# Short group's attention first, heads loaded one stage ahead, pooling in half pieces shared by GpSimd and VectorE

## Chip, cores, metric

One NeuronCore of a Trainium2 chip runs the whole layer as one launch. The metric is device time in microseconds (us).

## What is computed

Two request groups, a short one of 1024 tokens and a long one of 2048, go through one encoder layer with shared weights. Cut to what matters here:

```
z = (rmsnorm(x) * (1 + sc1) + sh1) @ w_in
c_q, c_kv, k_pe, u = split(z)                          # 384, 256, 32, 512 columns
q = rmsnorm(c_q) @ w_uq ; kv = rmsnorm(c_kv) @ w_ukv    # 8 heads: 64 + 32 (rotated) per query, 64 + 64 per key
att = softmax(q k^T / sqrt(96)) v                       # per head, within a group
pool = (mean of u over a window of 2, 4, 8 or 16 tokens - u) @ w_pool * pool_scale
x = x + g1 * (concat(att, pool) @ w_out)
y = rmsnorm(x + g2 * expert_choice_ffn(rmsnorm(x) * (1 + sc2) + sh2))
```

The window means divide by the number of tokens really in the window, so the first and last eight tokens of a sequence have factors of their own.

## The kernel before, in words

The stages follow each other with a barrier of all engines between them: modulation, `in_proj`, `latent_proj`, attention of the long group, attention of the short group, output weights and projection, routing, experts, final norm. Every float32 operand is split into a high and a low half, and a product is three matmuls. Between stages data goes through DRAM: `s_qn`, `s_qr`, `s_kn`, `s_v` hold the projected heads, `s_kr` the rotated key part that all heads share, `s_ut` the pooling input, `s_diff` the pooling result.

**`latent_proj` (L512)** works through six blocks of 512 tokens. A block has 16 items in the order `ORDER` (L526): four each of k, q and v, and two pairs r, t (the rotated query part). TensorE (PE) computes an item into one of eight PSUM banks, ScalarE (ACT) writes its high half, VectorE (DVE) its low half, and SyncE (SP) stores it. SP's queue (L674) is in program order, and so is the work that its transfers do. Beside this GpSimd (POOL) pools the windows in twelve jobs (L635), two per block: SP fetches a piece of 1024 tokens with its margins, POOL adds neighbours in one to four doublings, scales, subtracts, mends the ends, and SP stores the result at two places of a block (L712): `store_diff` waits until POOL has finished the job, then comes `fetch` of the job after next. Stores of items stand behind these waits in SP's queue.

**`attention` (L850)** is called for `g = 1` (long, two heads resident in SBUF, loops over four pairs) and then for `g = 0` (short, four heads resident, two rounds). SP first issues the loads of all resident heads (L985 to L992); PE waits for the first head's q and k (L1029, L1030). POOL writes three constant rows (L1224): row 96 of a head's tiles carries the row maxima through the score product. Then a pipeline runs in steps `s` of one 128-key tile against 512 queries: three score matmuls, `exp` and high half on ACT, low half on POOL, two value matmuls; PE also computes the next query block's maxima (`unit`), which DVE reduces. A block has 8 steps in the short group, 16 in the long one. After a block, at fixed steps of the next ones, its sums are finished: `sum_row` on ACT writes the row sums, SP's `fold` (L966) turns them by a small transfer, DVE's `inverse` (L1195) takes reciprocals and waits for that transfer, SP's `store_inverses` stores them, and `store` writes the output. In the short group `inverse` of block 0 comes at step 18 (`INV = 10`, L864). DVE executes in order, so everything behind `inverse` waits with it. SP's `body` (L994) starts only after the loads above it are issued.

Of the kernel before, what the change touches and what calls it, by code (L numbers as in the profile page):

```python
# [22 lines left out]
F32 = mybir.dt.float32  # L23
# [487 lines left out]

def latent_proj(nc, w, keep):  # L512
# [11 lines left out]
    SPAN = min(SEQS)  # L524
# [6 lines left out]
    PER = len(ORDER)  # L531
    SIMPLE = [i for i, (kind, _) in enumerate(ORDER) if kind in "kqv"]
    SLOT = {"q": 0, "r": NQ, "k": NQ + RT, "v": NQ + RT + KT}
    with ExitStack() as ctx:
# [10 lines left out]
        out = m.sb("out", [P, SLOTS, 2, BANK], F32R)  # L545
        prod = m.sb("prod", [P, 2, BANK])
# [22 lines left out]
        edge_in = m.sem("edge_in")  # L569
        pads_set = m.sem("pads_set")  # L570
# [47 lines left out]
        @block.gpsimd  # L618
        def _(pool):
            m.clear_last(pool)  # L620
            step = sequence(summed)
            pads = sequence(pads_set)

            def set_pads(n):

                first, last = ends_of(n)
                if first:
                    pads(nc.gpsimd.memset(u[:, n % 2, 0:PAD], 0.0))
                if last:
                    pads(nc.gpsimd.memset(u[:, n % 2, PAD + SPAN:], 0.0))  # L630

            for n in range(2):
                set_pads(n)
            pool.wait_ge(edge_in, 16)
            for n, (g, c, o) in enumerate(JOBS):  # L635
                x = u[:, n % 2]
                pool.wait_ge(u_in[n % 2], 16 * (n // 2 + 1))
                done = step(nc.gpsimd.tensor_tensor(sums[:, 0, 1:SPAN + 2 * PAD], x[:, 0:SPAN + 2 * PAD - 1],
                                                    x[:, 1:SPAN + 2 * PAD], ALU.add))
                for lev in range(1, c + 1):  # L640
                    r = 1 << (lev - 1)
                    lo, hi = 2 * r, SPAN + 2 * PAD - 2 * r + 1
                    src, dst = sums[:, (lev - 1) % 2], sums[:, lev % 2]
                    pool.wait_ge(summed, done)
                    done = step(nc.gpsimd.tensor_tensor(dst[:, lo:hi], src[:, lo - r:hi - r], src[:, lo + r:hi + r],
                                                        ALU.add))
                total = sums[:, c % 2]
                pool.wait_ge(summed, done)
# [3 lines left out]
                if first:  # L652
                    done = step(nc.gpsimd.tensor_tensor(ends[:, 0:PAD], total[:, PAD:2 * PAD], edge[:, c, 0:PAD], ALU.mult))
                if last:
                    done = step(nc.gpsimd.tensor_tensor(ends[:, PAD:], total[:, SPAN:SPAN + PAD], edge[:, c, PAD:], ALU.mult))
                done = step(nc.gpsimd.tensor_scalar(sums[:, (c + 1) % 2, PAD:PAD + SPAN], total[:, PAD:PAD + SPAN],
                                                    1.0 / WINDOWS[c], None, ALU.mult))
                pool.wait_ge(summed, done)
                a, b = PAD * first, SPAN - PAD * last
                done = step(nc.gpsimd.tensor_tensor(diff[:, n % 2, a:b], sums[:, (c + 1) % 2, PAD + a:PAD + b],  # L660
                                                    x[:, PAD + a:PAD + b], ALU.subtract))
                if first:
                    done = step(nc.gpsimd.tensor_tensor(diff[:, n % 2, 0:PAD], ends[:, 0:PAD], x[:, PAD:2 * PAD],
                                                        ALU.subtract))
                if last:
                    done = step(nc.gpsimd.tensor_tensor(diff[:, n % 2, SPAN - PAD:], ends[:, PAD:], x[:, SPAN:SPAN + PAD],
                                                        ALU.subtract))
                pool.wait_ge(summed, done)
                pool.sem_inc(diff_ready, 1)
                if n + 2 < len(JOBS):  # L670
                    set_pads(n + 2)

        @block.sync
        def _(sp):  # L674
# [9 lines left out]
            def fetch(n):  # L684

                g, c, o = JOBS[n]
                a, b = max(o - PAD, 0), min(o + SPAN + PAD, SEQS[g])
                if n >= 2:
                    sp.wait_ge(diff_ready, n - 1)
                sp.wait_ge(pads_set, sum(sum(ends_of(i)) for i in range(n + 1)))  # L690
# [9 lines left out]
            load(0)  # L700
            sp.dma_start(qraw[:], w["w_uq"][0].rearrange("(k p) n -> p k n", p=P)).then_inc(q_in, 16)
# [4 lines left out]
            for n in range(2):  # L706
                fetch(n)
            load(1)
            for b in range(NB):
# [21 lines left out]
                if b + 2 < NB:  # L731
                    sp.wait_ge(ready, (b + 1) * PER)
                    load(b + 2)
            for slot in range(SLOTS):
                sp.wait_ge(stored[slot], 16 * NB)
            for i in range(2):
                sp.wait_ge(diff_stored[i], 16 * len(JOBS) // 2)
# [69 lines left out]
        def _(dve):  # L807
            for n, (src, g, dst) in enumerate(pieces()):
                dve.wait_ge(w_hi_done, n + 1)
                nc.vector.scalar_tensor_tensor(dst[1], src, g, dst[0].bitcast(F32), ALU.mult,  # L810
                                               ALU.subtract).then_inc(w_lo_done, 1)
            dve.wait_ge(tabs_in, 2 * 16 * (P // ROPE))
            for b in range(NB):
# [3 lines left out]
                for n, (kind, i) in enumerate(ORDER):  # L817
                    q = b * PER + n
# [31 lines left out]
def attention(nc, w, keep, g):  # L850
# [18 lines left out]
    with ExitStack() as ctx:  # L869
        m = Pools(nc, ctx, f"att{g}")  # L870
        q = m.sb("q", [P, HU, 2, S], F32R)
        k = m.sb("k", [P, HU, 2, S], F32R)
        v = m.sb("v", [P, HU, NT, 2 * VD], F32R)
# [16 lines left out]
        kpe_in = m.sem("kpe_in")  # L890
# [58 lines left out]
        def _(sp):  # L949
            def load_qk(n, i):  # L950
                for dst, src in ((q[0:NOPE, i], w["s_qn"]), (q[NOPE:QK, i], w["s_qr"]), (k[0:NOPE, i], w["s_kn"])):
# [3 lines left out]
            def load_v(n, i):  # L955
                src = w["s_v"][t0:t0 + NT, :, bass.ds(n * 2 * VD, 2 * VD)]
                sp.dma_start(v[:, i].bitcast(F32), src.rearrange("t p c -> p t c")).then_inc(v_in[i], 16)
# [27 lines left out]
            load_qk(0, 0)  # L985
            for i in range(HU):
                sp.dma_start(k[NOPE:QK, i].bitcast(F32), w["s_kr"][:, :, tokens]
                             .rearrange("l r t -> r l t")).then_inc(kpe_in, 16)
# [18 lines left out]
            over_heads(sp, body)  # L1007
            store(ITERS, -1)
# [7 lines left out]
        def _(pe):  # L1016
            def unit(i, j, u):
# [3 lines left out]
                nc.tensor.matmul(m_ps[u % MB][:, :], q[0:QK, i, 0, at:at + P], k[0:QK, i, 0, cols(kb)],  # L1021
# [7 lines left out]
            pe.wait_ge(qk_in[0], 48)  # L1029
            pe.wait_ge(kpe_in, 16 * HU)  # L1030
# [6 lines left out]
            pe.wait_ge(rows_set, 4)  # L1037

            def scores(it, s):
# [6 lines left out]
                k_hi, k_lo = (k[0:QK + 1, h, l, kt * P:(kt + 1) * P] for l in range(2))  # L1046
                q_hi, q_lo = (q[0:QK + 1, h, l, cols(j)] for l in range(2))
# [4 lines left out]
            def values(it, s):  # L1052

                b, kt, h, j = at(s)
                if kt == 0:
                    if j == 0:
                        pe.wait_ge(v_in[h], 16 * (it + (1 if b >= 0 else 0)))
# [3 lines left out]
                for a in range(2):  # L1061
                    mm = nc.tensor.matmul(o_ps[b % 2][:, :], v[:, h, kt, :], pr[:, s % RING, a, :],  # L1062
# [11 lines left out]
            def body(it, last):  # L1074
                for s in range(PER):
# [5 lines left out]
                    if not (last and b == NG - 1):  # L1081
                        i, nj = after(b)
                        for u in UNITS[kt]:
                            if u == 0 and nj == 0:
                                pe.wait_ge(qk_in[i], 48 * (it + (2 if i == 0 else 1)))
# [12 lines left out]
        def _(act):  # L1098
            def max_row(i, j):
                nc.scalar.activation(q[QK:QK + 1, i, 0, cols(j)], m_ps[MB - 1][0:1, :], ACT.Copy).then_inc(row_done, 1)  # L1100
# [1153 lines left out]
def build(nc, w):  # L2254
# [6 lines left out]
    with ExitStack() as ctx:  # L2261
# [7 lines left out]
        latent_proj(nc, w, keep)  # L2269
        for g in (1, 0):  # L2270
            attention(nc, w, keep, g)
# [32 lines left out]
    "s_rden": [HEADS, TOKENS],  # L2304
    "s_diff": [DP // P, P, TOKENS],
# [61 lines left out]
```

## Time and profile before

| | |
|---|---|
| median of 3 runs | 4012.92 us (4011.62 to 4013.34) |
| the profiled execution | 4013.25 us, of which its span 4011.4 us |
| PE busy | 3628.6 us, 90% of the span |
| DVE, ACT, POOL busy | 2025.0, 1890.8, 1346.4 us |
| granted PE clock, mean | 0.946 |

Times in the trace run from the first instruction; the span ends with the last, and 1.85 us lie around it. The stages that the change touches stand at 489.7 to 700.6 us (`latent_proj`), 700.6 to 1519.2 us (long attention) and 1519.2 us to about 1755 us (short attention).

### The profile page before, as it was taken

Reading aid. Unit: us, or ns where it says so; the run is one execution under the profiler, and the core shown is the slowest. Engines: PE = TensorE matmul, PEld = TensorE weight load, DVE = VectorE, ACT = ScalarE, POOL = GpSimd, SP = SyncE. Lnnn points to the kernel's source line nnn. Section 1 sums busy time; section 2 is a strip of 40 time slices with the busy share of each in tenths; the row PEclk is TensorE's granted clock in tenths of the full one; section 3 lists DMA queues with packets and bytes.
Section 4 is the critical chain, followed back from the end, with each engine's and each line's share of the span. In section 5 each row is a group of like instructions: output and inputs, shape, how many; then the busy total and the mean of one; then the engine's idle time right before and its main releaser. Section 6 shows DMA issues by size and latency. Waiting matters only on the chain. (4 is left out here: it accounts for less than half of the span.)

```text
span 4011.4 us, 53884 instructions
## 1 busy us (share of the span) xinstructions
PE 3628.6 (90%) x18873; PEld 3093.1 (77%) x18873; DVE 2025.0 (50%) x3111; ACT 1890.8 (47%) x3258; POOL 1346.4 (34%) x1008
## 2 busy tenths in 40 slices
PE   8799897799999997969995599999999999999991
PEld 1799876577777775747773499999999999999991
DVE  0333254688888886842225554444444444444443
ACT  0444232688888895843321234344444434443433
POOL 0212067688988897852221000000000000000000
PEclk9899999899999998989996699999999999999995
DMA  7422399422222205235642344444444455444537
GB/s 253 146 100 94 110 364 365 87 43 43 43 44 43 44 6 114 60 105 153 181 146 89 105 137 152 147 145 150 148 152 152 156 157 157 152 146 151 157 100 272
DMA packets 350510, 538.89 MB, mean 134 GB/s; under 512 B 33782, under 2 KB 234742, under 8 KB 347386
## 3 DMA queue, kind: packets, MB, share of 16 engines
q1 hardware_dynamic: 326332, 448.60, 35.6%
q0 software_dynamic: 13824, 50.34, 5.2%
q10 hardware_dynamic: 10176, 37.75, 2.3%
q8 instruction: 90, 1.47, 0.2%
q14 instruction: 88, 0.72, 0.1%
HBM read 394.08 MB, written 142.46 MB: 134 GB/s over the span
## 5 line engine op out<-in xcount | busy, mean ns | idle before, releaser
L1229 POOL TENSOR_TENSOR att_pr<-att_e,att_pr 128x512 fp32r<-128x512 f32 x640 | 813.1, 1294 | 146.0 <-ACT att_pr L1116 135.6
L1982 POOL DMA_INDIRECT s_x<-moe_ye,moe_to_add x48 | 90.9, 1893 | 1440.1 <-DVE moe_ye L2169 1430.4
L1160 DVE TENSOR_REDUCE att_mx<-att_m_ps 128x1 f32<-128x512 f32 x640 | 423.2, 682 | 111.8 <-PE att_m_ps L1021 102.3
L2117 DVE TENSOR_TENSOR keep_wl<-keep_raw,keep_wh 128x1024 fp32r<-128x1024 f32 x380 | 440.0, 1221 | 34.1 <-ACT keep_wh L2071 34.1
L2071 ACT ACTIVATE keep_wh<-keep_raw 128x1024 fp32r<-128x1024 f32 x380 | 370.0, 1045 | 126.0 <-PE moe_d_ps L2048 126.0
L1062 PE MATMUL att_o_ps<-att_pr,att_v 128*128 128x512 f32 x1280 | 408.6, 400 | 4.8 <-POOL att_pr L1229 4.6
L1116 ACT ACTIVATE att_pr<-att_e 128x512 fp32r<-128x512 f32 x640 | 402.8, 629 | 18.3 <-issue 2.7
L1110 ACT ACTIVATE att_e<-att_s_ps 128x512 f32<-128x512 f32 x640 | 379.7, 593 | 64.7 <-PE att_s_ps L1050 20.1
L1182 DVE TENSOR_TENSOR att_acc_ps<-att_acc_ps,att_e 128x512 f32<-128x512 f32 x544 | 375.0, 689 | 17.2 <-ACT att_e L1110 11.0
L2097 ACT ACTIVATE moe_silu<-moe_a_ps 128x384 f32<-128x384 f32 x128 | 63.0, 492 | 645.7 <-PE moe_u_ps L2021 645.7
L2019 PE MATMUL moe_a_ps<-moe_xh,keep_wh 128*128 128x384 f32 x1024 | 345.9, 338 | 3.0 <-DVE moe_xl L2122 3.0
L2020 PE MATMUL moe_a_ps<-moe_xl,keep_wh 128*128 128x384 f32 x1024 | 345.2, 337 | 0.0
L2021 PE MATMUL moe_a_ps<-moe_xh,keep_wl 128*128 128x384 f32 x1024 | 345.0, 337 | 0.0
L2021 PE MATMUL moe_u_ps<-moe_xh,keep_wl 128*128 128x384 f32 x1024 | 344.1, 336 | 0.0
L2019 PE MATMUL moe_u_ps<-moe_xh,keep_wh 128*128 128x384 f32 x1024 | 344.1, 336 | 0.0
L2020 PE MATMUL moe_u_ps<-moe_xl,keep_wh 128*128 128x384 f32 x1024 | 344.1, 336 | 0.0
L2152 DVE TENSOR_TENSOR moe_hf<-moe_u_ps,moe_silu 128x384 f32<-128x384 f32 x128 | 71.3, 557 | 537.1 <-ACT moe_silu L2097 537.1
L2046 PE MATMUL moe_d_ps<-keep_wh,moe_hh 128*128 128x512 f32 x768 | 311.6, 406 | 0.0
L2048 PE MATMUL moe_d_ps<-keep_wh,moe_hl 128*128 128x512 f32 x768 | 303.9, 396 | 0.0
L2047 PE MATMUL moe_d_ps<-keep_wl,moe_hh 128*128 128x512 f32 x768 | 303.8, 396 | 0.0
L1062 PEld LDWEIGHTS att_o_ps<-att_pr,att_v 128*128 128x128 f32 x1280 | 242.4, 191 | 67.0 <-POOL att_pr L1229 12.3
L1021 PE MATMUL att_m_ps<-att_k,att_q 96*128 96x512 f32 x640 | 236.5, 411 | 58.7 <-DMA att_k<-s_kr 58.7
(266 smaller groups left out, 7720.9 us busy)
## 6 DMA issues: line engine op xcount, KB each, us to landing
keep_raw<-w_gate SPq DMA_DIRECT2D x64, 1024.0 KB, 5.3
keep_raw<-w_up SPq DMA_DIRECT2D x64, 1024.0 KB, 7.8
keep_raw<-w_down SPq DMA_DIRECT2D x64, 1024.0 KB, 6.7
ada_wa<-w_ada SPq DMA_DIRECT2D x12, 2048.0 KB, 9.8
s_ct<-inp_ct SPq DMA_DIRECT2D x24, 640.0 KB, 3.0
prj_ct<-s_ct SPq DMA_DIRECT2D x6, 2560.0 KB, 16.6
s_kn<-prj_out SPq DMA_DIRECT2D x24, 512.0 KB, 12.2
s_qn<-prj_out SPq DMA_DIRECT2D x24, 512.0 KB, 11.9
```

The source lines that it names most:

```text
L1062: mm = nc.tensor.matmul(o_ps[b % 2][:, :], v[:, h, kt, :], pr[:, s % RING, a, :], start=(kt == 0 and a == 0), stop=(kt == NT - 1 and a == 1))
L1110: nc.scalar.activation(e[:, s % RING, :], s_ps[s % 2][:, :], ACT.Exp, scale=SCALE).then_inc(exp_done, 1)
L1116: nc.scalar.activation(pr[:, s % RING, 0, :], e[:, s % RING, :], ACT.Copy).then_inc(hi_done, 1)
L1160: nc.vector.tensor_reduce(mx[:, u % CB, u // CB:u // CB + 1], m_ps[u % MB][:, :], AX, ALU.max).then_inc(max_part, 1)
L1182: step = nc.vector.tensor_tensor(acc_ps[:, :], acc_ps[:, :], e[:, s % RING, :], ALU.add)
L1229: nc.gpsimd.tensor_tensor(pr[:, s % RING, 1, :], e[:, s % RING, :], pr[:, s % RING, 0, :].bitcast(F32), ALU.subtract).then_inc(lo_done, 1)
L2019: nc.tensor.matmul(out, hi, xh[:, k, :], start=(k == 0), stop=False)
L2020: nc.tensor.matmul(out, hi, xl[:, k, :], start=False, stop=False)
L2021: mm = nc.tensor.matmul(out, lo, xh[:, k, :], start=False, stop=(k == KD - 1))
L2046: nc.tensor.matmul(out, h_hi, wh[:, c % 2, k, :], start=(k == 0), stop=False)
L2071: nc.scalar.activation(wh[:, s, part, :], raw[:, s, part, :], ACT.Copy).then_inc(w_hi_done, 1)
L2117: nc.vector.tensor_tensor(wl[:, s, part, :], raw[:, s, part, :], wh[:, s, part, :].bitcast(F32), ALU.subtract).then_inc(w_lo_done, 1)
```

## The change

1. Attention runs for the short group first, then the long one.
2. A tile `ahead0` takes q and k of the short group's first head; `latent_proj` loads it on SP's queue after the third block. A tile `ahead1` takes q, k and v of the first two heads of the long group; the short group's attention loads it behind its own three remaining heads, before its `body`. PE no longer waits at the start of either attention.
3. The constant rows are written to DRAM once (`s_rows`) and loaded per head, in place of POOL's memsets.
4. Pooling works on 24 pieces of 512 tokens, four places per block; POOL only adds (the last addition writes `diff`) and mends the ends, DVE scales and subtracts in one instruction per piece, ahead of the item at that place. The first two fetches come before the query weights.

```diff
+HEAD_LOADS = 8
+def load_heads(sp, w, g, n, heads, which, sem, values=True):
+    S = SEQS[g]
+    NT = S // P
+    tokens = slice(STARTS[g], STARTS[g] + S)
+    for i in which:
+        q, k, v = heads[i]
+        for dst, src in ((q[0:NOPE], w["s_qn"][:, n + i, :, tokens]), (q[NOPE:QK], w["s_qr"][:, n + i, :, tokens]),
+                         (k[0:NOPE], w["s_kn"][:, n + i, :, tokens]), (k[NOPE:QK], w["s_kr"][:, :, tokens])):
+            sp.dma_start(dst.bitcast(F32), src.rearrange("l r t -> r l t")).then_inc(sem, 16)
+        for dst, row in ((k[QK:QK + 1, 0], 1), (k[QK:QK + 1, 1], 0), (q[QK:QK + 1, 1], 0)):
+            sp.dma_start(dst.bitcast(F32), w["s_rows"][row:row + 1, 0:S]).then_inc(sem, 16)
+        if values:
+            sp.dma_start(v.bitcast(F32), ...).then_inc(sem, 16)
 def latent_proj(nc, w, keep):
-    SPAN = min(SEQS)
+    SPAN = BANK
+    JOBS_PER = len(JOBS) // NB
+    POINTS = [PER * (i + 1) // JOBS_PER - 2 for i in range(JOBS_PER)]
...
             def store_diff(n):
                 sp.wait_ge(diff_ready, n + 1)
+                sp.wait_ge(ends_ready, n + 1)
...
-                    if at in (PER // 3, 2 * PER // 3):
-                        n = 2 * b + int(at > PER // 2)
+                    if at in POINTS:
+                        n = JOBS_PER * b + POINTS.index(at)
                         store_diff(n)
                         if n + 2 < len(JOBS):
                             fetch(n + 2)
...
+                if b == SEQS[0] // BANK:
+                    sp.wait_ge(w_lo_done, ALL_PIECES)
+                    for slot in range(SLOTS):
+                        sp.wait_ge(stored[slot], 16 * b)
+                    load_heads(sp, w, 0, 0, head_tiles(keep, 0, None), range(1), ahead_in, values=False)
...
+            def difference(n):
+                dve.wait_ge(total_ready, n + 1)
+                nc.vector.scalar_tensor_tensor(diff[:, n % 2, a:b], diff[:, n % 2, a:b], 1.0 / WINDOWS[c],
+                                               u[:, n % 2, PAD + a:PAD + b], ALU.mult, ALU.subtract).then_inc(diff_ready, 1)
...
                 for n, (kind, i) in enumerate(ORDER):
+                    if n in POINTS:
+                        difference(JOBS_PER * b + POINTS.index(n))
 def attention(nc, w, keep, g):
-            load_qk(0, 0)
...
-            load_v(0, 0)
-            for i in range(1, HU):
-                load_qk(i, i)
-                load_v(i, i)
+            if g == 0:
+                load_v(0, 0)
+            for i in range(READY, HU):
+                load_heads(sp, w, g, 0, heads, (i,), rest_in[i])
+            if g == 0:
+                load_heads(sp, w, 1, 0, head_tiles(keep, 1, None), range(2), ahead_in)
...
-            pe.wait_ge(qk_in[0], 48)
-            pe.wait_ge(kpe_in, 16 * HU)
...
-            for row, value in ((k[QK:QK + 1, :, 0, :], 1.0), (k[QK:QK + 1, :, 1, :], 0.0), (q[QK:QK + 1, :, 1, :], 0.0)):
-                nc.gpsimd.memset(row.bitcast(F32), value).then_inc(rows_set, 1)
 def build(nc, w):
-        latent_proj(nc, w, keep)
-        for g in (1, 0):
-            attention(nc, w, keep, g)
+        with ExitStack() as ahead:
+            tile(ahead, "ahead0", [P, 4 * SEQS[0]], F32R, side="right")
+            latent_proj(nc, w, keep)
+            tile(ahead, "ahead1", [P, 2 * (4 * SEQS[1] + SEQS[1] // P * 2 * VD)], F32R, side="right")
+            for g in range(2):
+                attention(nc, w, keep, g)
```

SP's queue at the start of the short group's attention, before (`att_v`, `att_q`, `att_k` are the resident heads, `att_rden` the folded sums):

```order
L952 DMA att_q<-s_qn 64x2x1024
L952 DMA att_q<-s_qr 32x2x1024
L952 DMA att_k<-s_kn 64x2x1024
L957 DMA att_v<-s_v 128x8x128
L962 DMA s_att<-att_att 64x512
L973 DMA att_rden<-att_den 128x1x4
L980 DMA s_rden<-att_rden 128x4
```

and the end of the same loads now (`keep_ahead` is the tile filled ahead, `s_rows` the constant rows):

```order
L544 DMA att_v<-s_v 128x8x128
L540 DMA keep_ahead<-s_qn 64x2x2048
L540 DMA keep_ahead<-s_qr 32x2x2048
L540 DMA keep_ahead<-s_kn 64x2x2048
L540 DMA keep_ahead<-s_kr 32x2x2048
L542 DMA keep_ahead<-s_rows 1x2048 x3
L544 DMA keep_ahead<-s_v 128x16x128
L1030 DMA s_att<-att_att 64x512
L1041 DMA att_rden<-att_den 128x1x4
L1048 DMA s_rden<-att_rden 128x4
```

Two long heads (the second has the rows of the first) now stand between the short group's last head and the first store of results and the first fold.

In `latent_proj`, SP's queue after the third block holds, now, the first short head between the load of block 4 and the stores of block 3:

```order
L774 DMA s_qr<-prj_out 128x2x512
L721 DMA prj_ct<-s_ct 128x4x1280
L540 DMA keep_ahead<-s_qn 64x2x1024
L540 DMA keep_ahead<-s_qr 32x2x1024
L540 DMA keep_ahead<-s_kn 64x2x1024
L540 DMA keep_ahead<-s_kr 32x2x1024
L542 DMA keep_ahead<-s_rows 1x1024 x3
L774 DMA s_kn<-prj_out 128x2x512
```

Before, a store of `s_kn` followed the load of block 4 at once.

## Rows read from the trace of the kernel before

**Rows 1.** The page, busy time of each engine.

```profile
PE 3628.6 (90%) x18873; PEld 3093.1 (77%) x18873; DVE 2025.0 (50%) x3111; ACT 1890.8 (47%) x3258; POOL 1346.4 (34%) x1008
```

**Rows 2.** Busy times by stretch, latent projection: span; engines; PEclk, DMA share, GB/s.

```profile
515.00:545.00 30.00, 30.00 (x125) 24.59 (x125) 14.63 (x19) 7.11 (x12) 23.96 (x17) 0.93 1.03 400
545.00:549.00 4.00, 4.00 (x19) 3.34 (x18) 3.30 (x3) 2.69 (x5) 3.44 (x5) 1.00 0.31 122
549.00:680.00 131.00, 128.41 (x566) 106.02 (x566) 73.93 (x97) 38.00 (x66) 93.65 (x73) 1.00 1.03 398
685.00:690.00 5.00, 0.00 (x0) 0.00 (x0) 1.13 (x1) 0.31 (x1) 4.92 (x2) 0.50 0.11 43
690.00:700.00 10.00, 0.00 (x0) 0.00 (x0) 0.00 (x0) 0.00 (x0) 0.37 (x3) 0.50 0.83 316
```

**Rows 3.** Timeline of SP's queue, end of the latent projection.

```profile
679.68 1.17 SPq L730 DMA_DIRECT2D s_qn<-prj_out  x1
690.45 0.34 SPq L697 DMA_DIRECT2D s_diff<-prj_diff  x1
...
694.69 1.21 SPq L730 DMA_DIRECT2D s_qr<-prj_out  x1
700.57 0.66 SPq L952 DMA_DIRECT2D att_q<-s_qn  x1
```

**Rows 4.** Tile s_qn, the store issued at 679.68 us alone.

```profile
DMA to landing us min/median/max: 11.2/11.2/11.2
```

**Rows 5.** Timeline of PE around both attention starts.

```profile
680.70 0.39 PE L772 MATMUL prj_ps<-prj_ct,prj_wq 128*128 128x512 f32 x1
720.73 9.52 PE L1021 MATMUL att_m_ps<-att_k,att_q 96*128 96x512 f32 x16 [39.64 <-DMA att_k<-s_kr]
...
1513.58 0.63 PE L1071 MATMUL att_o_ps<-att_acc_lo,att_ones 128*1 128x512 f32 x1
1533.22 4.74 PE L1021 MATMUL att_m_ps<-att_k,att_q 96*128 96x512 f32 x8 [19.02 <-DMA att_k<-s_kr]
```

**Rows 6.** Timeline of SP's queue, short group: first and last head load, first results.

```profile
1519.17 0.65 SPq L952 DMA_DIRECT2D att_q<-s_qn  x1
...
1546.13 0.60 SPq L957 DMA_DIRECT2D att_v<-s_v  x1
...
1563.80 0.53 SPq L962 DMA_DIRECT2D s_att<-att_att  x1
1568.02 0.54 SPq L973 DMA_DIRECT2D att_rden<-att_den  x1
...
1576.30 1.09 SPq L962 DMA_DIRECT2D s_att<-att_att  x1
```

**Rows 7.** Timeline of DVE, the short group's first inverse.

```profile
1572.55 0.17 DVE L1197 RECIPROCAL att_rden<-att_rden 128x4 f32<-128x4 f32 x1
```

**Rows 8.** Busy times by stretch while heads load, columns as in Rows 2.

```profile
701.00:740.00 39.00, 17.30 (x40) 10.30 (x41) 13.23 (x23) 6.16 (x10) 13.37 (x6) 0.53 1.00 216
1521.00:1560.00 39.00, 24.59 (x83) 17.45 (x84) 18.64 (x32) 15.19 (x26) 21.96 (x14) 0.67 1.00 214
1533.00:1546.60 13.60, 11.42 (x25) 7.07 (x26) 7.10 (x13) 3.63 (x6) 2.56 (x2) 0.50 1.07 236
```

**Rows 9.** DMA of the stretch 1519 to 1562 us: packets, MB, share.

```profile
q1 hardware_dynamic: 5952, 8.39, 91.6%
```

**Rows 10.** Tile att_rden in the short group: DVE's waits for the fold; issue to landing.

```profile
  DMA att_rden<-att_den: 8.3, 4
...
DMA to landing us min/median/max: 1.4/2.0/5.6
```

**Rows 11.** Lines L638, L810 and L834: ns min/median/max, first and last start.

```profile
L638 POOL TENSOR_TENSOR prj_sums<-prj_u x12: 1917/1918/1923, 518.8 to 675.7; 128x1039 f32<-128x1039 f32 x12
...
L810 DVE SCALAR_TENSOR_TENSOR prj_wk<-prj_kvraw,prj_gain,prj_wk x2: 747/750/753, 496.2 to 497.6; 128x512 fp32r<-128x512 f32 x2
...
L834 DVE TENSOR_TENSOR prj_qf<-prj_prod x12: 692/931/2747, 529.4 to 681.9; 128x512 f32<-128x512 f32 x12
```

More of the change, by code:

```diff
@@ L509, in _, with head_tiles @@
                     mm.then_inc(ct_ready, 1)
+HEAD_LOADS = 8
+def head_tiles(keep, g, left):
+    S = SEQS[g]
+    NT = S // P
+    size = 4 * S + (NT * 2 * VD if g else 0)
+    heads = []
+    for i in range(2 if g else 1):
+        x = keep[f"ahead{g}"][:, i * size:(i + 1) * size]
+        heads.append((x[:, 0:2 * S].rearrange("p (l t) -> p l t", l=2), x[:, 2 * S:4 * S].rearrange("p (l t) -> p l t", l=2),
+                      x[:, 4 * S:].rearrange("p (t c) -> p t c", t=NT) if g else left and left[2][:, 0]))
+    if left:
+        q, k, v = left
+        heads += [(q[:, i], k[:, i], v[:, i + 1]) for i in range(3)]
+    return heads
+def load_heads(sp, w, g, n, heads, which, sem, values=True):
+    S = SEQS[g]
+    NT = S // P
+    tokens = slice(STARTS[g], STARTS[g] + S)
[7 more added lines that the diff above has]
+        if values:
+            sp.dma_start(v.bitcast(F32), w["s_v"][TILE0[g]:TILE0[g] + NT, :, (n + i) * 2 * VD:(n + i + 1) * 2 * VD]
+                         .rearrange("t p c -> p t c")).then_inc(sem, 16)
 def latent_proj(nc, w, keep):
@@ L545, in latent_proj @@
         out = m.sb("out", [P, SLOTS, 2, BANK], F32R)
+        rows = m.sb("rows", [P, 2, max(SEQS) // P], F32R)
         prod = m.sb("prod", [P, 2, BANK])
@@ L569, in latent_proj @@
         edge_in = m.sem("edge_in")
+        ahead_in = m.sem("ahead_in")
+        rows_set = m.sem("rows_set")
+        rows_stored = m.sem("rows_stored")
+        total_ready = m.sem("total_ready")
+        ends_ready = m.sem("ends_ready")
         pads_set = m.sem("pads_set")
@@ L630, in set_pads @@
                     pads(nc.gpsimd.memset(u[:, n % 2, PAD + SPAN:], 0.0))
+            for i in range(2):
+                nc.gpsimd.memset(rows[:, i, :].bitcast(F32), float(i)).then_inc(rows_set, 1)
             for n in range(2):
@@ L637, in _ @@
                 pool.wait_ge(u_in[n % 2], 16 * (n // 2 + 1))
[L638 to L648, printed above, removed]
                 if n >= 2:
@@ L651, in _ @@
                 first, last = ends_of(n)
[L652 to L669, printed above, removed]
+                for lev in range(c + 1):
+                    r = 1 << lev >> 1
+                    lo, hi = 2 * r + (lev == 0), SPAN + 2 * PAD - 2 * r + (lev > 0)
+                    src = sums[:, (lev - 1) % 2] if lev else x
+                    before, behind = (src[:, lo - r:hi - r], src[:, lo + r:hi + r]) if lev else (src[:, lo - 1:hi - 1], src[:, lo:hi])
+                    if lev == c:
+                        cut = slice(PAD - lo, PAD - lo + SPAN)
+                        nc.gpsimd.tensor_tensor(diff[:, n % 2], before[:, cut], behind[:, cut], ALU.add).then_inc(total_ready, 1)
+                    else:
+                        done = step(nc.gpsimd.tensor_tensor(sums[:, lev % 2, lo:hi], before, behind, ALU.add))
+                        pool.wait_ge(summed, done)
@@ new lines, in _ @@
+                if first or last:
+                    pool.wait_ge(total_ready, n + 1)
+                for here, at, e0 in ((first, 0, 0), (last, SPAN - PAD, PAD)):
+                    if here:
+                        done = step(nc.gpsimd.tensor_tensor(ends[:, e0:e0 + PAD], diff[:, n % 2, at:at + PAD],
+                                                            edge[:, c, e0:e0 + PAD], ALU.mult))
+                        pool.wait_ge(summed, done)
+                        done = step(nc.gpsimd.tensor_tensor(diff[:, n % 2, at:at + PAD], ends[:, e0:e0 + PAD],
+                                                            x[:, PAD + at:2 * PAD + at], ALU.subtract))
+                        pool.wait_ge(summed, done)
@@ L700, in _ @@
             load(0)
+            for n in range(2):
+                fetch(n)
             sp.dma_start(qraw[:], w["w_uq"][0].rearrange("(k p) n -> p k n", p=P)).then_inc(q_in, 16)
@@ L705, in _ @@
             sp.dma_start(edge[:].rearrange("p a b -> p (a b)"), w["k_edge"].partition_broadcast(P)).then_inc(edge_in, 16)
-            for n in range(2):
-                fetch(n)
             load(1)
+            sp.wait_ge(rows_set, 2)
+            sp.dma_start(w["s_rows"].rearrange("l (p c) -> p l c", p=P), rows[:].bitcast(F32)).then_inc(rows_stored, 16)
             for b in range(NB):
@@ L811, in _ @@
                                                ALU.subtract).then_inc(w_lo_done, 1)
+            def difference(n):
+                c = JOBS[n][1]
+                first, last = ends_of(n)
+                a, b = PAD * first, SPAN - PAD * last
+                dve.wait_ge(total_ready, n + 1)
+                nc.vector.scalar_tensor_tensor(diff[:, n % 2, a:b], diff[:, n % 2, a:b], 1.0 / WINDOWS[c],
+                                               u[:, n % 2, PAD + a:PAD + b], ALU.mult, ALU.subtract).then_inc(diff_ready, 1)
             dve.wait_ge(tabs_in, 2 * 16 * (P // ROPE))
@@ L870, in attention @@
         m = Pools(nc, ctx, f"att{g}")
-        q = m.sb("q", [P, HU, 2, S], F32R)
-        k = m.sb("k", [P, HU, 2, S], F32R)
-        v = m.sb("v", [P, HU, NT, 2 * VD], F32R)
+        left = None
+        if g == 0:
+            left = (m.sb("q", [P, HU - 1, 2, S], F32R), m.sb("k", [P, HU - 1, 2, S], F32R),
+                    m.sb("v", [P, HU, NT, 2 * VD], F32R))
+        heads = head_tiles(keep, g, left)
+        READY = HU if g else 1
+        q, k, v = ([h[a] for h in heads] for a in range(3))
         olo = m.sb("olo", [VD, BANK])
@@ L889, in attention @@
         acc_ps = m.ps("acc_ps")
-        kpe_in = m.sem("kpe_in")
+        rest_in = [m.sem(f"rest_in{i}") for i in range(HU)]
+        ahead_in = m.sem("ahead_in")
         qk_in = [m.sem(f"qk_in{i}") for i in range(HU)]
@@ L950, in load_qk @@
             def load_qk(n, i):
-                for dst, src in ((q[0:NOPE, i], w["s_qn"]), (q[NOPE:QK, i], w["s_qr"]), (k[0:NOPE, i], w["s_kn"])):
+                for dst, src in ((q[i][0:NOPE], w["s_qn"]), (q[i][NOPE:QK], w["s_qr"]), (k[i][0:NOPE], w["s_kn"])):
                     sp.dma_start(dst.bitcast(F32), src[:, bass.ds(n, 1), :, tokens]
@@ L1045, in scores @@
                 out = s_ps[s % 2][:, :]
-                k_hi, k_lo = (k[0:QK + 1, h, l, kt * P:(kt + 1) * P] for l in range(2))
-                q_hi, q_lo = (q[0:QK + 1, h, l, cols(j)] for l in range(2))
+                k_hi, k_lo = (k[h][0:QK + 1, l, kt * P:(kt + 1) * P] for l in range(2))
+                q_hi, q_lo = (q[h][0:QK + 1, l, cols(j)] for l in range(2))
                 nc.tensor.matmul(out, k_hi, q_hi, start=True, stop=False)
@@ L1056, in values @@
                     if j == 0:
-                        pe.wait_ge(v_in[h], 16 * (it + (1 if b >= 0 else 0)))
+                        loads = it - (0 if b >= 0 else 1) + int(g == 0 and h == 0)
+                        if not (isinstance(loads, int) and loads == 0):
+                            pe.wait_ge(v_in[h], 16 * loads)
                     if from_start(it, b - 2):
@@ L1084, in body @@
                             if u == 0 and nj == 0:
-                                pe.wait_ge(qk_in[i], 48 * (it + (2 if i == 0 else 1)))
+                                loads = it + (1 if i == 0 else 0)
+                                if not (isinstance(loads, int) and loads == 0):
+                                    pe.wait_ge(qk_in[i], 48 * loads)
+                                elif i >= READY:
+                                    pe.wait_ge(rest_in[i], 16 * HEAD_LOADS)
                             pe.wait_ge(max_part, (it * NG + b + 1) * NT + max(u - MB + 1, 0))
@@ L1099, in max_row @@
             def max_row(i, j):
-                nc.scalar.activation(q[QK:QK + 1, i, 0, cols(j)], m_ps[MB - 1][0:1, :], ACT.Copy).then_inc(row_done, 1)
+                nc.scalar.activation(q[i][QK:QK + 1, 0, cols(j)], m_ps[MB - 1][0:1, :], ACT.Copy).then_inc(row_done, 1)
             act.wait_ge(nmx_turned, 1)
@@ L2304 @@
     "s_rden": [HEADS, TOKENS],
+    "s_rows": [2, max(SEQS)],
     "s_diff": [DP // P, P, TOKENS],
```

20 lines of the change are left out of this document (13 added, 7 removed).

## Prediction, before the run

> **What bounds the kernel now.** I read the page first: PE is busy 90% of the span [rows 1], so time can only come out of the places where PE stands. The timeline of PE shows two of them inside the stages that the change touches [rows 5]. After the last projection at 680.7 us PE does nothing until 720.73 us, and the row puts 39.6 us of that down to the key's transfer; between the two groups it stands from 1514.2 to 1533.22 us, 19.0 us of it for the same transfer. The timelines of SP's queue split both gaps. The first one has a tail of the latent projection up to 700.57 us, where SP issues the first head load [rows 3], and then 20.2 us of loading. The second has 5.6 us in which the long group's last sums are stored, up to the first load at 1519.17 us [rows 6], and then 14.05 us of loading.
>
> The table by stretch tells what bounds the latent projection itself [rows 2]: from 515 to 680 us both PE and the 16 DMA engines are full. The DMA share is 1.03 at 398 to 400 GB/s, with one hole, 545 to 549 us, at 0.31. After 680 us PE is done and the DMA share falls to 0.11 while POOL finishes its last piece, for which SP waits until 690.45 us with five more stores behind it [rows 3]. That looks like 10 us lost to pooling, but it is not: the store issued just before, at 679.68 us, took 11.2 us to land [rows 4], until 690.9 us. The slowest of the 16 DMA engines was busy until then; the mean share of 0.11 says that the others had run dry. So the stage ends when the transfers end, and the pooling wait costs some 1.5 us of it.
>
> Head loads run at another rate: 216 GB/s in the long group and 214 GB/s in the short one, with the DMA share at 1.00 [rows 8]. That is a full queue at half the rate, and it prices every load that the change moves.
>
> **Loads taken out from in front of PE.** At the first attention, now the short one, PE starts when the stage starts: minus 20.2 us. Between the groups the same: minus 14.05 us. POOL's memsets ran beside the loads, so taking them out is worth nothing.
>
> **The first head inside the latent projection.** Its q and k are 1.57 MB: two halves of 96 rows of 4 KB, twice. At 215 GB/s that is 7.3 us of a DMA queue that is full there [rows 2, 8], so nothing covers it. Against that stand the 1.5 us above and perhaps some of the hole at 545 to 549 us, where 0.69 of 4 us, 2.8 us, was unused. Pooling itself moves off the bound: an addition of 1039 columns takes 1.918 us on POOL [rows 11], of half the columns about 0.96 us, and 24 pieces have 60 of them, 58 us beside 180. DVE gets 24 instructions of the kind that takes 0.75 us at 128x512 [rows 11], 18 us beside 93 us of work in those 180 [rows 2]; even at 2.75 us each, the longest that a DVE instruction with two SBUF inputs took there, they would fit. What doesn't fit so surely is the order: DVE now waits in its queue for POOL's sum, which waits for a fetch that was issued two places earlier, behind some 11 us of queued transfers [rows 4]. Two places are half a block, 15 us. I take plus 6 us for the stage, from minus 4 (both holes regained) to plus 18 (each wait on pooling also stops PE and lowers its clock once).
>
> **The new wait.** In the short group SP now has 41 transfers to issue before its `body`: v of the first head, three whole heads and two heads of the long group. Four short heads are 8.39 MB [rows 9]; without q and k of the first, 6.82 MB are left, and two long heads are another 8.39 MB: 15.2 MB. At 215 GB/s [rows 8] that is 70.7 us, plus 2 us from the first issue to the first bytes. The 15 rows of constants are 4 or 8 KB each; 216 GB/s over 16 engines is 13.5 GB/s for one, so a row costs at most 0.6 us and all at most 6 us; I take 1 us, as most will run beside other packets. The queue is empty about 73.7 us after the stage's start. The first `store` and the first `fold` are issued behind all that. A fold that has the queue to itself lands in 2.0 us, one behind a head's load in up to 5.6 us, and DVE stood 8.3 us in four such waits already [rows 10]: a small transfer does not pass a big one.
>
> When is the fold needed? Before, PE began the stage's work at 1533.22 us and DVE executed the first `inverse` at 1572.55 us [rows 5, 7], 39.3 us later, at step 18. SP had issued its last load by 1546.13 us and stored the first result at 1563.80 us [rows 6], so nothing was late. Now DVE reaches that instruction at 39.3 us and stands there until 74 us: 34.7 us. Behind it in DVE's queue are the reductions of the maxima and the running sums; with four buffers of `e` ACT can go three or four steps on, PE with it, then both stand. A step is 1.56 us (8 of them from 1563.80 to 1576.30 us, [rows 6]), so PE has some two of them in hand beyond what it has anyway, and I take off 3.5 us. A PE that has stood so long starts again at the low clock: after the 19 us gap the granted clock was 0.50, 1.2 GHz, for 13.6 us [rows 8], which is work for 6.8 us lost; 6.3 us, as part of it was waits. So plus 37.5 us: 31.2 of standing, 6.3 of clock. The bounds: 30 us (no clock loss) and 45 us (all rows on one engine).
>
> The DMA page of the Trainium skill says otherwise of the rate: DMA: Bandwidth & Descriptors, Anatomy of one DMA, fits a transfer's time as about 2.0 us plus its bytes at 436 GB/s, by which (an estimate from that page) the 15.2 MB would take 36.9 us and the fold would not be late. Its page SBUF — State Buffer, section on the DMA port swizzle, says why these loads may do less: partitions 0 to 63 reach only half of the 16 ports. The trace bears out the second page: 214 and 216 GB/s for tiles of 64 and 32 rows, 398 for those of 128.
>
> **The sum.** Plus 6, minus 20.2, minus 14.05, plus 37.5: plus 9.3 us on the profiled execution's 4013.25 us, 4022.5 us. That execution lies 0.3 us above the median of the runs, so 4022 us. The loads are not gone, they have moved in front of the first fold.
>
> **Rivals.**
> *The fold is not late.* If the prefetch drains within 39.3 us, or the fold passes it, the whole 37.5 us go and the time is 4013 + 6 - 34.2 = 3985 us. It decides at a rate of 15.2 MB in 37.3 us, 407 GB/s. For it speaks that 128-row tiles do reach 400 [rows 2]; against it that no head load of this trace does [rows 8]. 10%.
> *Pooling enters DVE's queue and stops the projection.* Each wait for a late fetch holds DVE, the PSUM banks fill, PE stands, and a stand of a few us costs the clock as well. The latent projection then grows by 18 us in place of 6: 4034 us. For it: 11 us of queue ahead of each fetch. Against it: half a block and eight banks of slack. 20%.
> *The latent projection takes the extra head for nothing,* since both holes close and SP no longer stands on pooling: minus 4 in place of plus 6, 4012 us, no change that a measurement tells. For it: the share of 0.11 after 685 us. Against it: the 11.2 us landing. 20%. With a stall at its lower bound of 30 us besides, it would be 4005.
> The change may also fail to do what it says, if the first head's load lands after the last store of the projection; the place in the queue, behind block 2 of 0 to 5, leaves more than 80 us, so I give it no share.
>
> **How the numbers follow.** The forecast has 50%, the rivals 10, 20 and 20. About 0.2% of the time, 8 us, is what a measurement of this kernel tells from no change: faster is below 4005, slower above 4021. Of the forecast's own spread (4012 to 4033) a little over half lies above 4021, the second rival nearly all, the third none. So slower 0.27 + 0.19 = 0.46, faster 0.10 + 0.05 of the third = 0.15, the rest 0.39. The range goes from 4003 (the third rival with a short stall) to 4041 (the second with rows of constants at their dearest), which leaves out the first rival and some of the far end. The forecast's own range is 4012 to 4033.
>
> **What would show it.** In the changed profile: PE's first `unit` of each attention within 1 us of the stage's start; DVE's `inverse` with one wait of about 35 us for the fold in the short group; SP's first `s_att` store only after the last long head's k has landed; DMA share 1.00 at about 215 GB/s over the first 70 us of that stage; the granted clock at 0.50 for some 14 us after the stand; the latent projection ending about 6 us later in spite of the shorter pooling, with DVE waits on POOL. The prediction is wrong if the wait for the fold is under 20 us, or if the latent projection ends before 695 us.

## The result, and the profile after

The changed kernel took **4019.51 us** (median of 20 runs, 4012.97 to 4027.41) against 4009.65 us for the kernel before (20 runs): ratio 1.0025, 95% interval 1.0019 to 1.0031. It is 9.9 us slower; the forecast was 4022, 9.3 us above the execution then profiled. The profiled execution took 4027.41 us, 8 us above its own median, so it is read by stage.

Timelines after, of SP's queue, PE and DVE, in the order of the program (start, duration, in brackets the idle time before):

```profile
705.24 0.39 SPq L1025 DMA_DIRECT2D att_v<-s_v  x1
...
736.06 22.05 SPq L540 DMA_DIRECT2D keep_ahead<-s_qn  x1
...
761.53 17.40 SPq L1030 DMA_DIRECT2D s_att<-att_att  x1
779.06 0.56 SPq L1041 DMA_DIRECT2D att_rden<-att_den  x1
```

```profile
705.27 1.19 PE L1089 MATMUL att_m_ps<-keep_ahead 96*128 96x512 f32 x2 [14.16 <-PEq L572]
...
784.09 0.80 PE L1089 MATMUL att_m_ps<-att_k,att_q 96*128 96x512 f32 x1 [37.37 <-DVE att_mx L1232]
...
966.24 1.19 PE L1089 MATMUL att_m_ps<-keep_ahead 96*128 96x512 f32 x2 [4.99 <-PEq L932]
```

```profile
743.68 0.69 DVE L1254 TENSOR_TENSOR att_acc_ps<-att_acc_ps,att_e 128x512 f32<-128x512 f32 x1
783.29 0.18 DVE L1269 RECIPROCAL att_rden<-att_rden 128x4 f32<-128x4 f32 x1 [38.91 <-DMA att_rden<-att_den]
```

The two waits for head loads [rows 5] are gone: PE starts 0.03 us after the first load is issued, and 5.0 us separate the groups where it was 19.0. In their place stands one wait of 37.37 us. DVE had come to its first inverse at 744.4 us, 39.1 us into the stage, and stood until the fold landed at 783.3. SP issued that fold only at 779.06: the issue of one load stood 22.05 us and that of the first result store 17.40 us. ACT had written the sums by 739.6 us, so 39.4 us passed before the fold was issued, and it landed 4.2 us behind that: the wait lies in front of the issue.

By stage, between the same SP issues and PE rows of both profiles, after minus before: latent projection (now from SP's issue at 491.97 us to the one at 705.24) 213.3 - 210.9 = +2.4; wait for the first head 20.2 to 0.0 = -20.1; short group's PE work 256.0 - 216.4 = +39.6; wait between the groups -14.0; long group's PE work 796.7 - 793.5 = +3.2; end of attention -0.4. That is +10.7. Work that the change doesn't touch gives +2.3 before 492 us and +1.2 after attention: +14.2 in all, the difference of the two profiled executions. The +3.2 is within scatter: the long group with its results on SP's queue took 786.6 to 796.7 us in eight profiles.

Busy times by stretch after (columns as in [rows 2]):

```profile
610.00:640.00 30.00, 22.77 (x97) 18.45 (x97) 10.64 (x17) 4.19 (x9) 13.38 (x16) 0.92 1.03 360
...
705.30:719.00 13.70, 11.74 (x30) 7.38 (x31) 7.75 (x15) 5.71 (x9) 2.65 (x3) 0.58 0.97 215
...
750.00:782.00 32.00, 0.00 (x0) 0.00 (x0) 0.00 (x0) 0.00 (x0) 0.18 (x1) 0.52 0.92 185
784.00:788.00 4.00, 3.91 (x9) 2.73 (x10) 4.00 (x8) 0.60 (x1) 0.00 (x0) 0.50 0.49 89
788.00:790.00 2.00, 2.00 (x11) 1.29 (x10) 1.69 (x4) 0.79 (x2) 0.00 (x0) 0.86 1.07 236
790.00:796.00 6.00, 6.00 (x28) 4.84 (x27) 4.24 (x7) 5.94 (x12) 5.31 (x5) 1.00 0.93 195
```

The heads load at 215 GB/s at first, as before [rows 8], and at 185 from 750 us on. The row of 610 to 640 us is the projection while the first head loads: PE is busy only 22.8 of 30 us. The missing 7.2 us are one stand:

```profile
638.06 0.80 PE L822 MATMUL prj_ps<-prj_wv,prj_ct 128*128 128x512 f32 x1 [7.24 <-DVE prj_out L910]
```

DVE had itself waited 13.4 us for POOL there, and POOL 13.2 us for the fetch of a pooling piece that SP issued behind the head.

### The profile page after: what moved, and what is told of

The parts are those of the page before. It is cut to its first block and busy times, and to the rows that moved or that the text cites. A ratio compares the mean times of both kernels' runs of the same rounds, so it can differ in the third digit from the quotient of the medians.

```text
span 4025.6 us, 54019 instructions
## 1 busy us (share of the span) xinstructions
PE 3636.8 (90%) x18873; PEld 3097.3 (77%) x18873; DVE 2022.9 (50%) x3135; ACT 1887.4 (47%) x3258; POOL 1275.6 (32%) x1010
## 5 line engine op out<-in xcount | busy, mean ns | idle before, releaser
L1130 PE MATMUL att_o_ps<-att_pr,keep_ahead 128*128 128x512 f32 x1024 | 328.8, 402 | 2.5 <-POOL att_pr L1299 2.5
L1130 PEld LDWEIGHTS att_o_ps<-att_pr,keep_ahead 128*128 128x128 f32 x1024 | 195.4, 192 | 50.1 <-POOL att_pr L1299 6.0
L1114 PE MATMUL att_s_ps<-keep_ahead 97*128 97x512 f32 x544 | 224.3, 412 | 3.9 <-issue 2.3
```

Of the source, the lines that this page charges most:

```text
L1130: mm = nc.tensor.matmul(o_ps[b % 2][:, :], v[h][:, kt, :], pr[:, s % RING, a, :], start=(kt == 0 and a == 0), stop=(kt == NT - 1 and a == 1))
```

## The experiments

Theory: the two long heads ahead of the first fold in SP's queue cost the short group 37 us. Rivals: its own three heads do it; the 16 engines are the limit, not the place in the queue; and for the projection, that DVE's waits on pooling hold its end.

**e1_late_pair** moves the long pair from in front of `body` into six pieces behind the folds:

```diff
-            if g == 0:
-                load_heads(sp, w, 1, 0, head_tiles(keep, 1, None), range(2), ahead_in)
...
                         store_inverses(it, b - 1)
+                    if g == 0 and last and 1 <= b <= 6:
+                        i, part = 0 + (b - 1) // 3, ((0, 2), (2, 4), (4, 8))[(b - 1) % 3]
+                        load_heads(sp, w, 1, 0, head_tiles(keep, 1, None), (i,), ahead_in, parts=part)
```

> The two long heads are loaded in six pieces behind the short group's blocks 8 to 13 instead of ahead of its first fold; all else as changed. If the two heads cause the stand: DVE's first inverse waits under 2 us for its fold, PE has no gap of 37 us, the time falls by 36 to 39 us against the changed kernel, to 3981 to 3984 us, and is 0.6% to 0.7% below the kernel before. If the short group's own three heads (6.8 MB, 32 us) already make the fold late: a wait of 10 us or more is left and the time stays above 3995 us. If the pieces now hold up later folds: the stand is replaced by six waits of 3 to 7 us, 4000 to 4015 us.

Measured: 3982.74 us, ratio 0.9934 (0.9921 to 0.9948). DVE's waits for folds in the short group:

```profile
DVE att_rden L1271 <- DMA att_rden<-att_den: 9.0, 7, 2.6
```

The longest is 2.6 us, the first inverse did not wait, and the short group's PE work is 219.0 us in place of 256.0. The stand is gone with the pair, so the group's own heads do not make the fold late.

**e2_no_pair** loads nothing of the long group ahead:

```diff
-        READY = HU if g else 1
+        READY = 1
...
-            if g == 0:
-                load_heads(sp, w, 1, 0, head_tiles(keep, 1, None), range(2), ahead_in)
...
+            if g:
+                pe.wait_ge(rest_in[0], 16 * (HEAD_LOADS - 1))
```

> The long group's heads are not loaded ahead at all: its first head loads at the start of its own stage, as before; all else as changed. If the two heads cause the stand: the stand of 37.4 us goes with its clock loss, and the long group's start costs 20 us of PE again, so 20 us below the changed kernel, about 4000 us (0.25% below the kernel before). If the short group's own heads cause it: the stand stays and the load comes on top, about 4040 us.

Measured: 4003.43 us, ratio 0.9989 (0.9980 to 0.9998), 16.1 us below the changed kernel. The short group took 217.9 us, without a stand, and PE waited at the long group's start:

```profile
947.21 1.22 PE L1088 MATMUL att_m_ps<-keep_ahead 96*128 96x512 f32 x2 [24.12 <-DMA keep_ahead<-s_rows]
```

So loading the pair ahead is worth 24.1 - 5.0 = 19.1 us and, placed as the change has it, costs 37: by itself a loss of 18 (16.1 measured).

**e3_one_late** leaves one long head in front and puts the other behind blocks 8 to 10 (`range(1)` in the preamble, `1 <= b <= 3` in the body).

> One long head stays ahead of the first fold, the other goes behind blocks 8 to 10. A queue in order at 215 GB/s: 4.19 MB less in front, the fold lands 19.5 us earlier, DVE's wait falls from 38.9 to 19 or 20 us, and the time lies 19 to 21 us below the changed kernel, near 4000 us. If the wait is not proportional to the bytes in front (a fixed cost of a full queue): a wait of over 30 us stays, within 8 us of the changed kernel; or it goes altogether, 36 us or more below.

Measured: 3999.56 us, ratio 0.9974 (0.9965 to 0.9983), 20 us below the changed kernel:

```profile
761.38 0.18 DVE L1273 RECIPROCAL att_rden<-att_rden 128x4 f32<-128x4 f32 x1 [18.40 <-DMA att_rden<-att_den]
```

38.91 to 18.40 us for one head less: 20.5 us, against 19.5 for 4.19 MB at 215 GB/s. The wait follows the bytes in front, and it passes before the issue: SP issued the fold 19.1 us after the sums were written, in place of 39.4, and it landed 4.0 us later, in place of 4.2.

**e4_act_queue** leaves all loads where the change has them and gives the results to ACT's queue:

```diff
-                sp.wait_ge(den_copied, it * NG + b + 1)
...
-                sp.dma_start(rden[:, b % 2, :], den[0:1, b % 2, :].rearrange("o (p c) -> o p c", c=CB)
+                act.wait_ge(den_copied, it * NG + b + 1)
...
+                act.dma_start(rden[:, b % 2, :], den[0:1, b % 2, :].rearrange("o (p c) -> o p c", c=CB)
...
                     finish(it, s, ROW, sum_row)
+                    finish(it, s, ROW, store)
+                    finish(it, s, ROW, fold)
+                    finish(it, s, INV + 2, store_inverses)
```

> Both attentions issue their result stores, folds and inverse stores on ACT's DMA queue; the loads, the two long heads among them, stay on SP's in the order of the change. If the place in SP's queue holds the fold: it lands 2 to 6 us after its issue while the heads still load, DVE waits under 5 us, and the time falls by 30 to 38 us less what ACT loses for three issues a block (0.5 us each, partly free): 3980 to 3998 us. If it is the 16 engines' bandwidth, whatever the queue: the fold is issued at 39 us of the stage and still lands only 20 us later or more, and the time stays above 4005 us.

Measured: 3984.22 us, ratio 0.9943 (0.9929 to 0.9957), as the theory's time has it, but not as its rows have it. From ACT's timeline, and the tile `att_rden` from 700 to 790 us (issue to landing):

```profile
738.47 0.56 ACTq L1150 DMA_DIRECT2D att_rden<-att_den  x1
```

```profile
DMA to landing us min/median/max: 5.8/7.2/14.1
```

The first fold passed the loads still queued on SP, yet took 14.1 us, not 2 to 6; PE stood 7.5 and 6.5 us, and the short group took 238.2 us. So both have a part. Of the 37.0 us that the pair costs the short group (256.0 against 219.0 in e1_late_pair), the other queue takes away 17.8, and 19.2 stay, 14.1 of them the two stands: measured by the group's time, the shared engines cost as much as the place in the queue. ACT's own issues are not the 19.2, since the short group took 219.1 us in e8_both below, with results on ACT's queue and the pair in pieces. The time is made good elsewhere. The long group, from its first product to its last, first here, then in e1_late_pair:

```profile
946.70:1720.40 773.70, 758.81 (x3264) 592.29 (x3264) 665.12 (x1120) 662.50 (x1152) 684.74 (x544) 0.99 0.17 35
```

```profile
929.70:1723.60 793.90, 768.38 (x3264) 599.92 (x3264) 664.79 (x1120) 670.75 (x1151) 689.78 (x544) 0.97 0.16 34
```

20.2 us less for the same products: 10.6 us fewer of idle time and 9.6 us less in the products, with the granted clock at 0.99 for 0.97. PE's waits for DVE's maxima in that stretch:

```profile
PE att_m_ps L1061 <- DVE att_nmx L1233: 7.3, 7, 1.3
```

```profile
PE att_m_ps L1096 <- DVE att_nmx L1238: 18.1, 7, 3.6
```

Where these waits come from, SP's queue shows at the places where the next head is loaded, six in the long group. One of them in e1_late_pair, and the same fold on ACT's queue in e4_act_queue:

```profile
1044.41 11.14 SPq L1031 DMA_DIRECT2D s_att<-att_att  x1
1055.74 0.53 SPq L1042 DMA_DIRECT2D att_rden<-att_den  x1
```

```profile
1069.03 0.51 ACTq L1150 DMA_DIRECT2D att_rden<-att_den  x1
```

Behind the head's loads the issue of the store stood 11.14 us (10.8 to 11.2 at the six places), and the fold, which follows it, was issued 4.7 us after its sums were written. On ACT's queue it was issued at once. It did not travel faster there: it landed 6.9 us after its issue, in place of 4.4. On SP's queue DVE waited 2.4 to 3.5 us at each of the six, PE stood as long, and behind four of them the granted clock was 0.50 for some 3.4 or 6.8 us, here the longer:

```profile
1059.70:1066.40 6.70, 5.89 (x16) 4.53 (x17) 2.28 (x5) 3.67 (x6) 2.65 (x3) 0.50 0.01 0
```

In e4_act_queue PE's stands at these places are 1.3 us or less, and the clock stays at 1.00 behind them. So the 20 us are short stands and the clock lost behind them.

The Trainium skill (DMA: Bandwidth & Descriptors, Issuing engines are not separate DMA queues) says that issuing on several engines will "only save the time on the sequencer it takes to initiate the DMA". The traces agree: the second queue saved time of issue, and no landing at these places became shorter. The Trainium skill adds there that this time is "usually small relative to the DMA itself"; here the issue of one store stood 11.14 us.

**e5_head_late** takes the first head out of the projection (its load moves to the start of the attention); **e6_old_pooling** besides restores the twelve pieces on POOL; **e7_three** gives the pooled input of e1_late_pair a third buffer:

```diff
-        u = m.sb("u", [P, 2, SPAN + 2 * PAD])
+        u = m.sb("u", [P, 3, SPAN + 2 * PAD])
...
-                        if n + 2 < len(JOBS):
-                            fetch(n + 2)
+                        if n + 3 < len(JOBS):
+                            fetch(n + 3)
```

> As e1_late_pair, but the short group's first head is loaded at the start of its own attention, not in the latent projection, which keeps the pooling in small pieces. If that head costs the projection its 7.3 us of a full queue: the projection (214 us on average in the five profiles that carry the head) shrinks to 206 to 208 us, PE waits 9 to 10 us at the start of the attention, and the time is 2 to 3 us above e1_late_pair's 3983 us, within its interval. If the projection takes the head for nothing: 213 to 215 us of projection, and 9 to 10 us above e1_late_pair.

> As e5_head_late, with the pooling of the kernel before (twelve pieces of 1024 tokens, all on POOL). If the transfers bound the projection and pooling costs some 1.5 us of it: projection 209 to 212 us (210.9 in the kernel before), 2 to 5 us above e5_head_late where that has 207. If the small pieces bring 10 us, all that the projection stood after 680 us: 217 us or more. If they harm, because DVE waits 59 us for POOL: 203 us or less, faster than e5_head_late.

> As e1_late_pair, with three buffers for the pooled input, so that a piece is fetched three places ahead, and POOL waits for the store of the result only before its last addition. If the transfers bound the projection: DVE's waits on POOL fall from 59 us to under 25, PE ends earlier, and the projection stays within 2 us of e1_late_pair's 215.4 us. If DVE's waits set its end: it shrinks by 5 to 10 us, and the time falls to 3973 to 3978 us.

| | projection, us | time, us | ratio |
|---|---|---|---|
| e1_late_pair | 215.4 | 3982.74 | 0.9934 (0.9921 to 0.9948) |
| e5_head_late | 210.5 | 3992.64 | 0.9951 (0.9937 to 0.9965) |
| e6_old_pooling | 212.7 | 3996.16 | 0.9969 (0.9956 to 0.9981) |
| e7_three | 213.6 | 3981.62 | 0.9930 (0.9918 to 0.9942) |

The projection with the head took 213.3, 215.4, 213.8, 214.0 and 214.6 us in five profiles, 214.2 on average. Without it 210.5: the head costs 3.7 us there, half the 7.3, between the two cases expected of e5_head_late. That is good to some 2 us, since profiles of one and the same projection differ by as much (210.9 in the kernel before, 209.2 in e9_before_act below). PE then waited 11.5 us for the head at the start of the attention, not 9 to 10; 11.5 - 3.7 = 7.8 us, and the time is 9.9 us above e1_late_pair (6.8 by the ratios), with intervals that overlap. Small pieces against large ones are worth 2.2 us in the two single profiles (e6_old_pooling); that is within the scatter, and their times overlap, so that it is small is shown, its sign is not. e7_three missed its row: DVE's waits on POOL fell from 59.9 us in e1_late_pair (16 waits) to 46.3 only (12 waits), since POOL now waited 52.7 us for the stores of results. The projection stayed within 2 us, as the transfers' theory has it, though PE's longest stand for DVE fell from 8.6 to 3.0 us; but so small a cut of DVE's waits says little against the rival.

**e8_both** is e7_three with results on ACT's queue as in e4_act_queue, and with one wait that paces the six pieces; **e9_before_act** is the kernel before with results on ACT's queue. The wait in e8_both:

```diff
                     if g == 0 and last and 1 <= b <= 6:
+                        sp.wait_ge(rden_done, it * NG + b)
```

> e7_three with the results of both attentions on ACT's queue as in e4_act_queue; the six pieces of the long heads are paced by waits for DVE's inverses. In e4_act_queue the long group took 773.7 us against 793.9 in e1_late_pair: if that is the folds no longer queued behind head loads, it adds to what e7_three has: 3956 to 3964 us, 1.1% to 1.3% below the kernel before. If the 20 us came from the order of e4_act_queue otherwise (the pair loaded early, with nothing left on SP): the long group stays near 794 us and the time within 4 us of e7_three's 3982 us.

> The kernel before, with the results of both attentions on ACT's queue and nothing else changed. If folds behind head loads in one queue cost the long group 20 us there too (it took 793.5 us from its first product to its last): 774 us, 18 to 26 us below the kernel before, some 3984 to 3992 us. If only the changed kernel's order had that cost: within 4 us of the kernel before.

Measured: e8_both **3964.43 us, ratio 0.9888** (0.9872 to 0.9904), the fastest here; e9_before_act 3994.89 us, 0.9967 (0.9956 to 0.9978). The long group took 773.8 us in e8_both, and in e9_before_act:

```profile
719.20:1492.90 773.70, 760.12 (x3264) 593.99 (x3264) 665.26 (x1119) 664.60 (x1152) 684.85 (x544) 0.99 0.19 41
```

So the kernel before already paid 20 us for results behind head loads in one queue: at its six places the issue of the store stood 10.5 to 12.6 us, and the fold came 4.3 to 6.4 us after its sums. Its short group took 219.0 us in e9_before_act in place of 216.4. By the medians the total gained 13 us, less than the 18 to 26 expected, which were reckoned from the execution first profiled (4013.25 us); that one lies 5 us above the kernel before in these runs (4008.15 us), and the spans of the two profiled executions differ by 19.0 us. e8_both ends 0.4 us above its range; the long group of e7_three had taken 786.6 us, so 13 us were left to gain there and not 20.

## Why the prediction was right

- **Loads in front of PE**, -20.2 and -14.05: measured -20.1 and -14.0. Right, and both rows were in the profile of before.
- **The new wait**, +37.5: measured +39.6 against before and 37.0 between the changed kernel and e1_late_pair. The place (the first fold), the instruction that waits (`inverse`, due 39.3 us in, reached at 39.1) and the cause (bytes ahead in SP's queue) were right; e1_late_pair and e3_one_late show it. The bytes act through the issue: they held SP, so that the fold was issued late and then landed in 4.2 us. The two parts of the term were mis-sized and cancel. The fold landed 78.0 us after the stage's start, not 73.7: from 750 to 782 us the engines moved 185 GB/s at a share of 0.92, and of the 3.5 us taken off for PE's lead over DVE 1.5 showed; PE stood 37.4 us, not 31.2. And the "6.3 of clock" was carried over from the start of a stage: after this stand the granted clock was 0.50 (1.2 GHz) for some 4 us, about 2 us of work.
- **The latent projection**, +6: measured +2.4 in the profile of the changed kernel, +3.3 over the five, good to some 2 us. The term that was too dear is "At 215 GB/s that is 7.3 us of a DMA queue that is full there [rows 2, 8], so nothing covers it": the head cost about half.
- **The rivals.** "The fold is not late" is out. "Pooling enters DVE's queue and stops the projection": DVE waited 58.6 us in 16 waits, one of which stopped PE for 7.24 us, and PE made its last product 198.8 us after the stage's start in place of 191.0; but the stage grew by 2.4 us and not by 18. The mechanism is there once, behind the head's load; its price is not. In both kernels the stage ends with the stores, 14 to 20 us after PE's last product, which would cover the stand; that this is the reason was not tried. "The head for nothing" is out by its number: +2.4 to +3.3 lie nearer to the forecast's +6 than to its -4.
- **The rate.** The prediction gives 214 and 216 GB/s as the rate of tiles of 64 and 32 rows. The stretches of [rows 8] also hold v, a quarter of their bytes, whose tiles have 128 rows. From 1519 to 1562 us of the trace of before, the median packet of 4 KB (q and k) took 307 ns, where one of 4 KB into or out of 128 rows took 159 ns in the projection; the packets of v, 512 B, took 35 ns, about as long a byte as those of q and k. So half the rate is right for the sum, but the number of rows does not explain it for v. The fit of the Trainium skill that the prediction sets against this rate (DMA: Bandwidth & Descriptors, Anatomy of one DMA) is given there for transfers issued by GpSimd; SP issues these.
- **The sum**, +9.3, against +9.9 measured: some 3 us too much for the projection and about 2 too little for the short group. The four terms measured +7.9 by the two profiles; the rest of the +9.9 lies within the scatter of work that the change leaves alone. So the agreement to 0.6 us is partly luck. One case, the third rival with a short stall, stands in it as 4005 us and as 4003. The forecast came from pricing the moved loads where they land.

## What to carry to other kernels

A prefetch is paid for by what is queued behind it on the same engine. Before moving loads ahead, list the first small transfer behind them, when it is needed, and the bytes in front divided by the rate that such loads reach in the trace: 15.2 MB ahead of a transfer due in 39 us cost more than the 34 us that the prefetch saved. Look at how long the issues themselves stand, since the small transfer was late before it was issued. Cut the prefetch into pieces that drain between two such transfers, and give the small ones a queue of their own: together (e8_both, whose third buffer showed no gain by itself) that turned 0.25% slower into 1.1% faster.

## What the runs showed of the hardware

- Loads that have not drained hold the issuing engine too: SP's issue of a load stood 22.05 us and that of a 64x512 store behind them 17.40 us, where others take about 0.6. In the long group the issue of such a store stood 10.5 to 12.6 us behind each head's loads, before the change as well.
- A small transfer on a second queue passes the first queue's backlog but is no longer quick: 14.1 us while the heads loaded in e4_act_queue, 2.0 us as a median in the kernel before [rows 10].
- After 37.4 us of standing the granted clock came back from 0.50 to 1.00 (1.2 to 2.4 GHz) within 6 us of the first product; after the 19 us gap before it took 13.6 us [rows 8]. In both stretches PE was busy most of the time; what makes the difference was not tried.
- Stands of PE of 2.5 to 3.6 us were enough to be followed by a clock of 0.50: behind four of six in e1_late_pair's long group, for some 3.4 or 6.8 us.
